# Channel mixers of a decoder trunk: a weight-stationary up projection with feature-major result, and a first projection that starts on pieces

## The reference

```python
def swiglu(x, w_in, w_out):
    gate, up = jnp.split(x @ w_in, 2, axis=-1)
    return (jax.nn.silu(gate) * up) @ w_out
...
x = layer_norm(ALPHA * x + 0.5 * swiglu(x, ffn1_w_in[l], ffn1_w_out[l]), ln_gain[l, 0], ln_bias[l, 0])
```

## Time and profile before

| what | us |
|---|---|
| median of 3 runs | 1039.26 |
| lowest, highest | 1039.02, 1041.03 |
| the profiled execution, whole | 1038.74 |
| its span (first to last instruction) | 1036.6 |
| PE busy | 1005.6 (97%) |
| DVE busy | 653.4 (63%) |
| ACT busy | 495.7 (48%) |

### The profile page before, as it was taken

The page is one execution under the profiler, slowest core; times in us unless marked ns, Lnnn a source line. Parts: engine busy times, 40 slices in busy tenths (PEclk is TensorE's granted clock), DMA queues, the critical chain, the costliest instruction groups (busy, mean ns, idle before and its releaser), DMA issues.

```text
span 1036.6 us, 12902 instructions
## 1 busy us (share of the span) xinstructions
PE 1005.6 (97%) x4748; PEld 832.8 (80%) x4748; DVE 653.4 (63%) x837; ACT 495.7 (48%) x548; POOL 33.0 (3%) x61
## 2 busy tenths in 40 slices
PE   5999999999999999999999999999999899999997
PEld 4888888887788888888888888888888778888885
DVE  4564454886777545567954455878877876454555
ACT  4455454336547444452534335286777335334340
POOL 2000000000210000000000000000000100000000
PEclk9999999999999999999999999999999999999999
DMA  9765555553655665574476565453433346555531
GB/s 311 267 203 186 188 179 199 180 187 107 235 202 182 226 201 176 189 230 134 164 242 196 172 198 184 143 168 117 132 111 122 104 147 231 186 184 202 166 118 40
DMA packets 133108, 184.29 MB, mean 178 GB/s; under 512 B 5840, under 2 KB 112992, under 8 KB 132944
## 3 DMA queue, kind: packets, MB, share of 16 engines
q1 hardware_dynamic: 130160, 173.56, 50.6%
q0 software_dynamic: 2624, 9.66, 2.6%
q10 hardware_dynamic: 288, 0.59, 0.2%
HBM read 182.73 MB, written 1.05 MB: 177 GB/s over the span
## 4 chain that ended last, share of the span: by engine, by line
PE 89%; DVE 6%; ACT 3%; DMA 1%; issue 1%; SPq 0%; DVEq 0%; ACTq 0%
PE psum L1197 27%; PE psum L1199 27%; PE psum L1198 27%; DVE w_lo L663 2%; PE psum L1263 2%; PE psum L1545 2%; DMA raw<-in_ffn_w_in 1%; ACT w_hi L371 1%; PE psum L1192 1%; PE psum L1532 1%; PE psum L1533 1%; DVE stats L682 1%; DVE x_tok L680 1%; ACT L553 0%; ACT arena L501 0%
## 5 line engine op out<-in xcount | busy, mean ns | idle before, releaser
L663 DVE TENSOR_TENSOR w_lo<-raw,w_hi 128x2048 fp32r<-128x2048 f32 x164 | 374.9, 2290 | 182.1 <-ACT w_hi L371 181.7
L1197 PE MATMUL psum<-w_hi,xT_hi 128*128 128x512 f32 x960 | 382.5, 398 | 5.9 <-DVE xT_lo L670 4.2
L1199 PE MATMUL psum<-w_hi,xT_lo 128*128 128x512 f32 x960 | 375.2, 391 | 0.0
L1198 PE MATMUL psum<-w_lo,xT_hi 128*128 128x512 f32 x960 | 375.1, 391 | 0.0
L371 ACT CAST w_hi<-raw 128x2048 fp32r<-128x2048 f32 x164 | 311.8, 1908 | 14.7 <-DMA raw<-in_ffn_w_in 10.4
L1197 PEld LDWEIGHTS psum<-w_hi,xT_hi 128*128 128x128 f32 x960 | 181.0, 189 | 43.9 <-DVE xT_lo L670 5.1
L1199 PEld LDWEIGHTS psum<-w_hi,xT_lo 128*128 128x128 f32 x960 | 180.8, 188 | 39.1
L1198 PEld LDWEIGHTS psum<-w_lo,xT_hi 128*128 128x128 f32 x960 | 181.1, 189 | 35.5
L381 ACT ACTIVATE ffn_tok<-psum 128x256 f32<-128x256 f32 x88 | 33.8, 384 | 241.4 <-PE psum L1199 241.3
L1197 PE MATMUL psum<-w_hi,hT_hi 128*128 128x512 f32 x352 | 138.3, 393 | 0.0
L1199 PE MATMUL psum<-w_hi,hT_lo 128*128 128x512 f32 x352 | 137.2, 390 | 0.0
(11 more groups left out here) (159 smaller groups left out, 580.2 us busy)
## 6 DMA issues: line engine op xcount, KB each, us to landing
raw<-in_ffn_w_in SPq DMA_DIRECT2D x176, 512.0 KB, 4.7
raw<-in_ffn_w_out SPq DMA_DIRECT2D x88, 512.0 KB, 4.0
raw<-in_c_w_in SPq DMA_DIRECT2D x32, 512.0 KB, 4.8
raw<-in_ab_w_in SPq DMA_DIRECT2D x16, 512.0 KB, 4.8
raw<-in_ab_w_o SPq DMA_DIRECT2D x8, 512.0 KB, 3.7
raw<-in_c_w_o SPq DMA_DIRECT2D x8, 512.0 KB, 4.1
ln_gb<-in_ln_gain POOLq DMA_DIRECT2D x6, 512.0 KB, 4.9
ln_gb<-in_ln_bias POOLq DMA_DIRECT2D x6, 512.0 KB, 6.1
```

Source lines behind the costliest of these rows:

```text
L663: nc.vector.tensor_tensor(w_lo[:, n % RING], raw[:, n % RAW], w_hi[:, n % RING].bitcast(F32), ALU.subtract).then_inc(lo_ready, 1)
L1197: nc.tensor.matmul(dst, a_hi, b_hi, start=first, stop=False)
L1198: nc.tensor.matmul(dst, a_hi, b_lo, start=False, stop=False)
L1199: return nc.tensor.matmul(dst, a_lo, b_hi, start=False, stop=last)
```

## The change

**The projection in the loop (chunks 2 to 9 of each mixer).** `project_fold` makes the weights the stationary operand, in blocks of 128 features, and x the moving one. `xT_hi` and `xT_lo` now lie side by side in one tile (`xT_both`), so that one matmul with `w_hi` streams 512 columns, 256 of `hi` and 256 of `lo`; a second one with `w_lo` streams only the 256 columns of `hi`, into the first half of the same bank. A bank thus holds 128 features x (256 tokens, and 256 sums still to be added to them). j counts the two feature blocks of a chunk, g gate and up: G holds j = 0, T holds j = 1. DVE adds the halves (`fold_sums`, a TENSOR_REDUCE of 512 to 256, four in a chunk), ACT applies silu, DVE multiplies (`fold_hidden`), and the product is feature-major as it stands: `hidden_T` goes from the loop, and ACT and DVE split it out of SBUF (`fold_hid_hi`, `fold_hid_lo`). Chunks 0, 1 and 10 stay token-major.

**Waits.** Since j = 1 uses T, PE waits there for `hidT_lo` of the chunk before; before the change the first that waited for it was `down`, behind the whole projection. `ffn_hidT` of chunk 1 goes ahead of the split of unit s0+7 on ACT and DVE, and ahead of `lower_bound(1)` on DVE.

**The start.** x comes in four DMAs (tile t, half h) and units 0 to 2 in four pieces each, all on SP's queue; each piece is split and multiplied by itself. PE runs 6, 5 and 2 dummy matmuls (`warm`) ahead of and between the first steps. GpSimd's table loads start after unit 4 is split rather than after x has landed.

```diff
+            def fold_silu(name, c, j):
+                act.wait_ge(gate_summed, c * 2 + (SILUS[name] * 2 * N_FOLD + j - 3))
+                nc.scalar.activation(ffn_tok[:, 0, j], ffn_tok[:, 0, j], ACT.Silu).then_inc(silu_ready, 1)
...
                 split_hi(s0 + 6)
+                ffn_hidT(name, 1, 1)
                 split_hi(s0 + 7)
-                ffn_hidT(name, 1, 1)
...
-                        for t in range(TT):
-                            split_hi(n + t, i)
-                            ffn_silu(name, t, c, G[t])
+                        for j in range(2):
+                            split_hi(n + j, i)
+                            fold_silu(name, c, j)
                         split_hi(n + 2, i)
-                        ffn_hidT(name, c, par)
+                        fold_hid_hi(name, c, par)
...
+            def fold_sums(name, c, j):
+                dve.wait_ge(chunk_done[j], c + (CHUNKS_BEFORE[name] + 1))
+                dve.wait_ge(hidT_lo, c + SILUS[name] * NH)
+                for g, done in enumerate((gate_summed, up_summed)):
+                    nc.vector.tensor_reduce(ffn_tok[:, g, j], U[j][g].rearrange("p (a f) -> p f a", a=2), AX.X,
+                                            ALU.add).then_inc(done, 1)
...
+            def hi_pass(dst, slot, cs, kk):
+                return nc.tensor.matmul(dst, w_hi[:, slot, cs], xT_both[:, kk].rearrange("p a f -> p (a f)"),
+                                        start=kk == 0, stop=kk == KB - 1)
+            def lo_pass(dst, slot, cs, kk):
+                return nc.tensor.matmul(dst[:, 0:SEQ], w_lo[:, slot, cs], xT_hi[:, kk], start=False, stop=False)
...
+                        for g in range(2):
+                            cs = slice(k * 512 + g * FC + j * P, k * 512 + g * FC + (j + 1) * P)
+                            dst, passes = U[j][g], (hi_pass, lo_pass) if kk == 0 else (lo_pass, hi_pass)
+                            for one in passes:
+                                ins = one(dst, slot, cs, kk)
...
                 with pe.Fori(0, NPAIR) as i:
                     for par in range(2):
                         n, c = s0 + 5 + 3 * par, i * 2 + (2 + par)
-                        for t in range(TT):
-                            pe.wait_ge(hid_ready, c * 2 + (hid - 1 + t))
-                            project(n, i, t, G[t])
+                        pe.wait_ge(hid_ready, c * 2 + (hid - 1))
+                        project_fold(n, i, 0)
+                        pe.wait_ge(hidT_lo, c + SILUS[name] * NH)
+                        project_fold(n, i, 1)
                         for t in range(TT):
                             down(name, n + 2, i, c - 1, (1 + par) % 2, t, False, False)
-                        hidden_T(name, ((c * 2, ffn_tok[:, 1, 0]), (c * 2 + 1, ffn_tok[:, 1, 1])))
...
+            def program_start():
+                warm(6)
+                pe.wait_ge(const_landed, 16)
+                first_xT(0, 0)
+                warm(5)
+                first_piece(0, 0, 0)
+                first_xT(1, 0)
+                warm(2)
+                for k in range(PIECES):
+                    for t in range(TT):
+                        if k + t:
+                            first_piece(0, k, t)
+                    if k == 1:
+                        for t in range(TT):
+                            first_xT(t, 1)
+                for t in range(TT):
+                    for k in range(PIECES):
+                        first_piece(1, k, t)
```

More of the change, by code:

```diff
@@ L279, in load_halves @@
             def load_halves(n, n_static, w, kh, parts, g0, c):
-                if not (type(n) is int and n < RAW):
-                    sp.wait_ge(lo_ready, n - RAW + 1)
+                sp.wait_ge(lo_ready, n - RAW + 1)
                 dst = raw[:, n_static % RAW].rearrange("p (k g f) -> p k g f", k=4, g=2)
@@ L287, in load_halves, with load_piece, load_x, load_first @@
                                  ).then_inc(raw_landed[n_static % RAW], 16)
+            def load_piece(n, k, w):
+                p = PIECES * n + k
+                sp.dma_start(raw[:, n, k * 512:(k + 1) * 512].rearrange("p (g f) -> p g f", g=2),
+                             w.rearrange("(k p) (g f) -> p k g f", p=P, g=2)[:, p % KB, :, bass.ds((p // KB) * FC, FC)]
+                             ).then_inc(piece_landed[p], 16)
+            def load_x(t, h):
+                cs = slice(h * 512, (h + 1) * 512)
+                sp.dma_start(x_tok[:, t, cs], x[0, t * P:(t + 1) * P, cs]).then_inc(x_landed[t][h], 16)
+            def load_first(w):
+                load_x(0, 0)
+                load_piece(0, 0, w)
+                load_x(1, 0)
+                for k in range(1, PIECES):
+                    load_piece(0, k, w)
+                load_x(0, 1)
+                load_x(1, 1)
+                for n in range(1, RAW):
+                    for k in range(PIECES):
+                        load_piece(n, k, w)
             def load_rows(n, n_static, w, c):
@@ new lines, in fold_hidden, with fold_hid_lo @@
+            def fold_hidden(name, c, j):
+                dve.wait_ge(silu_ready, c * 2 + (2 * SILUS[name] * NC + j + 1))
+                dve.wait_ge(up_summed, c * 2 + (SILUS[name] * 2 * N_FOLD + j - 3))
+                nc.vector.tensor_tensor(ffn_tok[:, 1, j], ffn_tok[:, 1, j], ffn_tok[:, 0, j], ALU.mult
+                                        ).then_inc(hid_ready, 1)
+            def fold_hid_lo(name, c, par):
+                dve.wait_ge(hidT_hi, c + (SILUS[name] * NH + 1))
+                nc.vector.tensor_tensor(hT_lo[:, par], hid_T, hT_hi[:, par].bitcast(F32),
+                                        ALU.subtract).then_inc(hidT_lo, 1)
@@ L1201, in _, with project @@
             FIRST, SECOND = range(4), range(4, KB)
-            def project(n, i, t, g, blocks=range(KB)):
+            def project(n, i, t, g, blocks=range(KB), landed=False):
                 for kh in range(2):
@@ L1208, in project @@
                         continue
-                    pe.wait_ge(lo_ready, n + kh + 1 if i is None else i * RING + (n + kh + 1))
+                    if not landed:
+                        pe.wait_ge(lo_ready, n + kh + 1 if i is None else i * RING + (n + kh + 1))
                     slot = (n + kh) % RING
@@ new lines, in warm, with first_xT @@
+            def warm(times):
+                pe.wait_ge(warm_ready, 1)
+                for _ in range(times):
+                    nc.tensor.matmul(Y[1][1][:, 0:P], arena[:, 0:P], arena[:, 0:P], start=True, stop=True)
+            def first_xT(t, h):
+                pe.wait_ge(x_landed[t][h], 16)
+                if h:
+                    pe.wait_ge(xT_lo_ready, t + 1)
+                for k in range(4):
+                    ins = nc.tensor.transpose(T[t][:, k * P:(k + 1) * P],
+                                              x_tok[:, t, (4 * h + k) * P:(4 * h + k + 1) * P], ident[:])
+                ins.then_inc(xT_done, 1)
@@ new lines, in first_piece @@
+            def first_piece(n, k, t):
+                if k == PIECES - 1:
+                    pe.wait_ge(lo_ready, n + 1)
+                else:
+                    pe.wait_ge(piece_lo, (PIECES - 1) * n + k + 1)
+                pe.wait_ge(xT_lo_ready, 2 * (n % 2) + t + 1)
+                project(n - n % 2, None, t, G[t], (4 * (n % 2) + k,), landed=True)
+            def program_start():
[6 more added lines that the diff above has]
+                warm(2)
+                for k in range(PIECES):
+                    for t in range(TT):
[5 more added lines that the diff above has]
+                for t in range(TT):
+                    for k in range(PIECES):
+                        first_piece(1, k, t)
```

221 lines of the change are left out of this document (148 added, 73 removed).

## The result

The changed kernel takes 1042.83 us (median of 18 runs), the kernel before 1039.82 in the same sessions. The ratio is 1.0039, its 95% interval 1.0027 to 1.0051: the change costs 0.4%, 4.1 us. (The ratio is an estimate from all the runs; the two medians by themselves lie 3.0 us apart.) The forecast was 1041. The profiled execution took 1042.44 us, its span is 1040.6, against 1038.74 and 1036.6 before.

A forecast was written before the change was run, and what follows sets the result against it. PE's stream was taken as the bound (97% busy). 1038.74 - 8.8 (projection) + 13.3 (waits) + 1.7 (clock) - 4.5 (start) = 1040.4 us, so 1041 for the median; range 1029 to 1049.

The forecast's parts named there:

- the likeliest case: Whole kernel: the four terms bring 1038.74 to 1040.4 us, 1041 for the median; chance 0.47, own range 1036 to 1046.
- projection of 32 chunks: Loop on PE: narrow matmuls at 120 ns make a chunk 16.54 us against 16.82, -8.8 us in all; ends -19 and +6.
- waits in F0, F1, F2: Chunk 3 of these mixers: PE waits for ACT and DVE, +13.3 us together, 9 of it three 3.0 us waits.
- clock: PE behind the 3.0 us waits: one fall to 1.2 GHz, +1.7 us; ends 0 and 5.
- start: Kernel's beginning: x in pieces brings F0's loop to about 40 us from 44.52, -4.5 us; ends -2 and -7.
- (a): Loop projection: narrow matmul at load pace or in proportion, 110 to 113 ns, another 7 to 10 us off, 1032; chance 0.20.
- (c): Loop projection: alternating widths keep the pace disturbed, 135 ns per narrow matmul, 1056 us; halfway, at 128, 1049; chance 0.15.
- doesn't depend on how late DVE is: Chunk 3's 3.0 us wait for hidT_lo: set by unit 10 standing ahead of hT_hi and hT_lo, not by DVE's lateness.
- the ends 0 and 5: Clock term's bounds in us around +1.7, the upper one for three falls.
- L of 40: First matmul of F0's loop: expected at about 40 us, against 44.52 before.
- Rival (d): Start: clock and DMA issue eat the gain, +3, 1044 us; chance 0.06.
- Rival (b): Chunk 3: the waits don't come, because the split of unit 9 or 10 finds room, 1026 us; chance 0.12.

The follow-up runs named there:

- e1_order: The changed kernel with the hidden-tile copies (hT_hi on ACT, hT_lo on DVE) ahead of the split of a chunk's third weight unit: 1035.15 us, ratio 0.9948 to the kernel before.
- e1_relaxed: The changed kernel with PE's wait for the previous chunk's hT_lo moved from the projection's second half to ahead of `down`: 1032.58 us, ratio 0.9923 to the kernel before.
- e3_args_strong: The changed kernel, its hT_lo wait kept, with F1's three bound subtractions on DVE ahead of the tables and unit 7's split: 1041.29 us, ratio 1.0008.
- e1_fold_only: The kernel before with only the new projection loop and the new order ahead of it, beginning as it was: 1048.24 us, ratio 1.0077.
- e2_no_warm: The kernel before with the new beginning alone, less its dummy matmuls: 1037.72 us, ratio 0.9983 to the kernel before.
- e2_args: e1_relaxed with F1's three bound subtractions on DVE ahead of the tables and unit 7's split: 1031.38 us, ratio 0.9912 to the kernel before.

## Why the prediction was right, by its steps

The time came within 2 us and inside the range, the likeliest case's sum was a small loss, and the chances were open between faster and slower. Three of the four terms were off, by 3.5, 0.8 and 1.8 us: the first two made the kernel slower than forecast, the third faster. That the sum came so near is partly luck: with the start as forecast the same kernel would be some 1.8 us further off. In the profiled execution:

| term | forecast | measured | worked out from |
|---|---|---|---|
| projection of 32 chunks | -8.8 | -5.3 | 32 x (16.65 - 16.816) |
| waits in F0, F1, F2 | +13.3 | +13.1 | excess of chunks 2 and 3 over 2 x 16.65: 5.47, 5.07, 5.46; less 3 x 0.13, the excess of F3's first chunk, and less the falls |
| clock | +1.7 | +2.5 | 21.74 and 21.66 in F0 and F2, less 20.44 in F1 |
| start | -4.5 | -6.3 | 38.27 - 44.52 |
| sum | +1.7 | +4.0 | the profiled executions differ by 3.7; the 0.13 us of each mixer's first chunk stands in no term |

**The projection** is the term that was mis-sized most, by 3.5 us. I took 120 ns for the narrow matmul, and it is 117; but I left the wide one at 226.7, the pace of a long row of wide ones. It doesn't stand in such a row any more, and it takes 233. The pair is 350 for 347, which makes 0.10 us of the 0.11 that the chunk is over 16.54. Rivals (a), 110 to 113, and (c), 128 and up, fall by their prices. But (c)'s thought, that alternating widths keep the pace disturbed, fits the spacings above, in the wide matmul and not in the narrow one where I looked for it; my answer that it settles within a chunk holds for the old loop, where 72 wide ones stand in a row. The Trainium skill's page "TensorE: Matmul & The Clock Gate", section "Back-to-back issue gap", gives 109 ns for the isolated gap at 256 columns; the trace has 117 and doesn't agree.

**The waits** were right in place and size, and in the order as a cause; one step was wrong. (The three mixers' sums as I wrote them, 4.2, 5.0 and 4.3, add up to 13.5, not 13.3.) Counted from the loop's start the split of unit 8 begins on DVE at 12.9 us in F0, 13.9 in F1 and 13.0 in F2, forecast 13.0, 13.9 and 13.1. The idle time is 2.7 where I said 3.0; that a wait then costs 3.0 is luck, since the slower restart behind it wasn't in my sum. That it comes from the order, a weight split ahead of hT_lo on both engines, and from the lost cover of `down`, is shown by e1_order and e1_relaxed, each of which takes 10 to 12 us away. I wrote that this wait "doesn't depend on how late DVE is". That step failed: F3 has the order and no wait (the prediction itself expects nothing there, since no work stands ahead of that loop), and in F1 the wait fell to 1.05 when ACT's split of unit 8 came 3.5 us earlier (e3_args_strong). It takes both, the order and work ahead of the loop that has made ACT and DVE late. F2's wait for the product is 0.16. F0's isn't in the list, but PE's first matmul of chunk 3 starts 0.48 us behind the one before it, where 0.23 is usual: 0.25 for the forecast 0.3.

**The clock** fell twice, not once, and a fall cost 1.25 rather than 1.7: three waits alike gave two falls. In e1_fold_only a window behind F0's wait shows 1.00, behind F1's 0.53 and behind F2's 0.51. The runs spread with the mean clock as well: 1041.15 to 1042.0 us at 0.995, about 1042.7 at 0.993, 1047.75 and 1048.91 at 0.988. I had the ends 0 and 5 for this. Falls outside these mixers take part in that: the profiled execution of e1_relaxed has one in C that e1_order's lacks, which is why the first took longer as a whole, 1033.90 us for 1033.43, with 1.2 us less in the chunks: from F2's loop to F3's, over C, it took 1.7 us more. The skill's section "HAM oscillation — how this bites in real kernels" names idle gaps as what puts the clock back; the changed kernel and e1_fold_only agree in two of three cases each, and which of equal gaps does it can't be told from the gap.

**The start** was undersized by 1.8 us. The first piece came at 7.02 (forecast 7.5) and the second at 9.91 (10.5), and PE ran at 2.4 GHz from 6 us on, with the first chunks at 0.227 a matmul. My L of 40 had kept some half-rate time and small waits that didn't come. Rival (d) fell: even without the dummy matmuls (e2_no_warm) the start is 2.6 us ahead of the old one.

Rival (b), 1026, was the kernel without the waits. e1_relaxed is that kernel as far as the large waits go, at 1032.6: the rival's price had the projection's error of 3.5 us in it, and took the small waits for gone as well, while chunks 2 and 3 of F0, F1 and F2 are still 4.4 us over 6 x 16.65 there. It would also have needed an edit that the change doesn't make.

## What to carry to other kernels

When a restructured loop drops work that used to stand between a product and its consumer (here the transposes and a `down`), look at what each wait now protects. The one on hT_lo was for `down`, stood 5.6 us too early, and alone turned a gain of 0.8% into a loss of 0.4%. A loop that runs with slack can still lose in its first chunks: one-off work ahead of it is paid there, and how long ACT waits there for DVE decides how much: moving three instructions of DVE took 1.9 us off (e2_args). And when a stream of equal matmuls becomes one of mixed widths, price each of them anew, not only the one whose shape is new.

## What was not expected of the hardware

- A 512-column fp32r matmul took 226.7 ns in a long row of its like. Behind narrow ones it took some 231 in the old form, for the first six to ten of a row, and some 233 in the new projection, in each of three orders of its matmuls. A 256-column one took 117.
- Reordering 16 matmuls so that 8 in a row accumulate into one bank made a chunk 0.11 us slower, 16.76 for 16.65.
- Idle times of 2.69 to 2.73 us were followed by 1.2 GHz in F0 and F2 and not in F1, at equal length; in e1_fold_only F1 and F2 had it and F0 not.
- With 22 dummy matmuls and four transposes from 1.05 us on, the clock was at 2.4 GHz at the first projection at 7.02. The dummies are worth 3.3 us at the place in AB with POOL's loads late; with these early (239.63 and 240.23) they are worth 0.6.
